# Sixty-four experts on one core: router, slots and first gathers moved under the shared expert, and the residual rows loaded first at the end

## The chip, the core and the metric

The kernel runs on one core of one Trainium2 chip. The metric is the device time of one execution in microseconds, the median of the runs. TensorE (PE) multiplies, VectorE (DVE) and ScalarE (ACT) work elementwise, GpSimd (POOL) and SyncE (SP) issue DMAs, each from a queue of its own, and all transfers run on the core's 16 DMA engines. Each engine runs its own instruction stream in order, and streams meet at semaphores.

## The reference

Two blocks follow each other on 512 tokens of width 1024, in fp32. The first has a state-space mixer, a convolution mixer and two dense feed-forwards, the second a hybrid mixer, cross attention to 256 memory rows, and a mixture of experts. The change touches only the second block from its cross attention on:

```python
x = layer_norm_2(DEEPNORM_ALPHA * x + xa, ln2_g[l], ln2_b[l])
ff = moe_ffn(x, w_router, router_bias, w_exp_gu, w_exp_down, w_sh_gu, w_sh_down)
x = layer_norm_2(DEEPNORM_ALPHA * x + ff, ln3_g[l], ln3_b[l])

def moe_ffn(x2d, ...):
    scores = sigmoid(x2d @ w_router)                     # 512 x 64
    sel = scores + router_bias                           # the best 4 of 8 groups, then the best 8 experts
    w = scores[top_idx] / sum(...) * 2.5
    # every expert: swiglu(rows of its tokens, w_exp_gu[e], w_exp_down[e]) * w, added to its tokens
    return routed + swiglu(x2d, w_sh_gu, w_sh_down)      # one shared expert for all tokens
```

An expert's gate/up weights are 1024 x 512 (2048 KB), its down weights 256 x 1024 (1024 KB).

## The kernel before, in words

Everything is written by hand, engine by engine; the order of the code is the order of each engine's stream. `phase_end` is a barrier: every engine signals that it is drained and waits for the others. SP's loads of weights go through two ring buffers (`wring0`, `wring1`), a load being issued when PE has finished the tiles that used the buffer (`tile_done`). PE's results of a tile go to one of four PSUM banks, which ACT evacuates (`take`, `take_raw`, with `tile_evac`).

The mixture begins behind barrier 16, with the normalised state transposed (features on partitions) in `hT`. PE multiplies it with the router weights (line 1472), turns `hT` back to token rows (`turn`, 8 tiles), then does the shared expert's gate/up (`proj_pairs`, 4 tiles), its down product (`proj`, 8 tiles) and turns the residual `ALPHA*hT + shared` from `sq` to rows (8 tiles). ACT computes the sigmoid (2107), waits for DVE's choice of experts and weights, writes the weights' high part (2109), and then copies the row tiles into two buffers `tokb`, which POOL writes to DRAM tables one by one, each write waiting for the one before: first `xtab` (the rows that experts gather), later `rest` (the residual rows). A barrier (17) follows. Then PE multiplies the 0/1 choice mask with a triangle and with ones, to get each token's position in its expert's list (lines 1489 to 1494), then another barrier (18), then for experts 0 to 2 the slots: DVE makes a one-hot matrix (`m_onehot`), PE multiplies it with the table `rinfo` of token numbers, ranks and weights (`m_idx`), DVE converts the result to indices (`m_conv`), and POOL gathers the expert's rows, at most 112 (`m_gather`).

The expert loop has one step per expert (`m_step`). Every fp32 operand is split into a high and a low fp32r part, and a product is three products of parts. PE turns the gathered rows (`m_turn`), ACT and DVE split them (`m_xhi`, `m_xlo`) and the gate/up weights (`m_ghi`, `m_glo`, four slices each), PE multiplies (`m_gu`, 24 matmuls), ACT and DVE apply silu and the token's weight (`m_silu`, `m_act`), and so on to the down product (`m_down`) and POOL's scatter of the result (`m_scatter`) to row rank x 512 + token of `ytab`: an expert that is a token's r-th writes to rank r's 512 rows. Weight buffers are four deep: `wgu` (here `wring0`, `wring1`, `uT`, `sq`) and `wdn` (in the arena). SP loads expert e + 4 as soon as expert e's product is done (`expert_gu`, `expert_down`). The high part of even experts' gate/up weights is held in `hT`.

At the end eight ranks and the residual rows are read back (2048 KB each) and added per token. SP issues them in the order 0, 1, 2, 3, 4, rest, 5, 6, 7, each when its buffer is free and all experts that can write to it have scattered (`all_added`). DVE adds ranks 1, 2, 3 and rest onto rank 0; PE adds ranks 4, 5, 6, that sum and rank 7 in PSUM, by products with the identity (`add_rank`, line 1600). The last layer norm and the output follow, 128 rows at a time.

Of the kernel before, what the change touches and what calls it, by code (L numbers as in the profile page):

```python
# [28 lines left out]
ALU = mybir.AluOpType  # L29
# [3 lines left out]
P = 128  # L33
# [107 lines left out]
def build(nc, A, out):  # L141

    ctx = ExitStack()
    with ctx:
# [79 lines left out]
        def pc(name, i=0):  # L224
# [190 lines left out]
        NE, CAP, NTOK, RING, TOPK = 64, 112, T, 8, 8  # L415
        MORE = -(-(NTOK - CAP) // CAP)
# [9 lines left out]
        wgu = (wring[0], wring[1], flat(uT), flat(sq))  # L426
        wgu_lo = (wlo[0], wlo[1], flat(uT_r), flat(sq_r))
# [39 lines left out]
        ranks = carve(TC * NE)  # L467

        rows4 = lambda a: a.rearrange("p (c d) -> p c d", d=D)
        start_of = lambda a, n: arena[:, a:a + n]  # L470
        rank_rows = [rows4(r) for r in (
            wring[0][:, :], wring[1][:, :], flat(uT), flat(hT), flat(sq),
            start_of(moe_top, 4 * D), start_of(10 * D, 4 * D), start_of(moe_top + SLOT, 4 * D))]
        rest_rows = rows4(start_of(2 * D, 4 * D))
        g3, b3 = [[raw[2 * k + half][:, 0:512] for half in range(2)] for k in range(2)]
        fin = [rank_rows[0][:, c, :] for c in range(TC)]
# [25 lines left out]
        iot_and_rot = sem("iot_and_rot")  # L502
# [26 lines left out]
        first_ranks, second_ranks = sem("first_ranks"), sem("second_ranks")  # L529
# [25 lines left out]
        gw_in = [sem(f"group_weights_in{q}") for q in range(4)]  # L555
# [20 lines left out]
        def _(sp):  # L576
# [179 lines left out]
            sp.dma_start(memk, A["mem_2"][0].rearrange("(c p) d -> p c d", p=P)).then_inc(in3, 16)  # L756
            tiles.inc(NK)
# [4 lines left out]

            slot(4, two_cols(A["w_sh_gu_2"][0], 0, 256, 256))
# [3 lines left out]
            sp.dma_start(wrt, A["w_router_2"][0].rearrange("(k p) n -> p k n", p=P)).then_inc(in3, 16)  # L767
            sp.dma_start(rbias, A["router_bias_2"][0].partition_broadcast(P)).then_inc(in3, 16)
            sp.dma_start(sc_c2, A["shape_constants"]).then_inc(in3, 16)
# [45 lines left out]
            def load_rest():  # L815
                sp.dma_start(rest_rows, rest.rearrange("(c p) d -> p c d", p=P)).then_inc(second_ranks, 16)
# [11 lines left out]
            with sp.If(crowded > CAP):  # L828
                for e in done:
                    sp.wait_ge(done[e], 19)  # L830
# [2327 lines left out]
```

## Time and profile before

| | us |
|---|---|
| median of 3 runs | 3196.72 |
| lowest, highest | 3195.97, 3205.72 |
| the profiled execution | 3201.49 |
| its span, first to last instruction | 3199.8 |
| PE, DVE, ACT busy | 2880.4, 2120.2, 1456.7 |

The profile is one execution. Engine rows give the start, the duration, the line, the operation with output<-inputs, and in brackets the engine's idle time before it and what ended that. An x behind a row is a count of merged instructions; an fp32 matmul makes two records. PEclk is the granted share of TensorE's full clock (1.00 is 2.4 GHz, 0.50 is 1.2). DMA share is the mean busy share of the 16 DMA engines.

### The profile page before, as it was taken

To read this page: it belongs to the slowest core of one execution; us is meant where nothing else is said; L and a number is where in the kernel's file an instruction comes from. 1 tells how busy PE (TensorE), PEld (TensorE's weight loads), DVE (VectorE), ACT (ScalarE), POOL (GpSimd) and SP (SyncE) were. 2 spreads that over 40 slices of the span, in tenths; PEclk is the share of its full clock that TensorE was granted. 3 is DMA by queue.
4 is the path that set the end of the run, shared out by engine and by line. 5 is a ranking of instruction groups with operands and counts; after the bars stand their busy time and mean duration, and the time that the engine had idled before them with its cause. 6 is when DMAs were issued, how large, how long until landed. Compare 5 with 4: busy or idle time off the path is not lost.

```text
span 3199.8 us, 36554 instructions
## 1 busy us (share of the span) xinstructions
PE 2880.4 (90%) x12311; PEld 2100.3 (66%) x12311; DVE 2120.2 (66%) x3288; ACT 1456.7 (46%) x2217; POOL 168.6 (5%) x165
## 2 busy tenths in 40 slices
PE   8999899999989899999888998888865999999996
PEld 6777777887868578878664333554444777777773
DVE  4778546776279667762554997431424999999985
ACT  5665432223245532232233554331323887777771
POOL 0000000000000000000000000000000322222220
PEclk9999999999999999999898998989976999999998
DMA  3222222322321022323221000203006999999996
GB/s 106 61 56 68 87 79 79 105 79 81 90 79 53 27 92 92 105 65 107 64 79 50 1 1 24 72 24 118 27 31 240 348 337 342 350 344 340 336 341 263
DMA packets 294316, 419.34 MB, mean 131 GB/s; under 512 B 33643, under 2 KB 178467, under 8 KB 294211
## 3 DMA queue, kind: packets, MB, share of 16 engines
q1 hardware_dynamic: 276675, 380.20, 35.9%
q0 software_dynamic: 17536, 37.78, 3.4%
q8 instruction: 61, 1.00, 0.1%
q14 instruction: 44, 0.36, 0.0%
HBM read 407.42 MB, written 35.65 MB: 138 GB/s over the span
## 4 chain that ended last, share of the span: by engine, by line
PE 61%; SPq 17%; DVE 11%; ACT 4%; DMA 4%; issue 3%; DVEq 0%; ACTq 0%; POOLq 0%
PE tp L1045 37%; SPq L779 12%; PE tp L1004 5%; SPq L786 4%; PE tp L1098 2%; PE tp L1099 1%; PE tp L1100 1%; PE tp L1358 1%; PE mp L1078 1%; PE mp L1064 1%; DVE wring_r L2235 1%; DMA arena<-ytab 1%; PE mp L1273 1%; PE mp L1272 1%; PE mp L1274 1%
## 5 line engine op out<-in xcount | busy, mean ns | idle before, releaser
L1045 PE MATMUL tp<-sq_r,arena_r 128*128 128x512 f32 x1152 | 461.2, 400 | 43.4 <-DVE uT_r L2248 25.7
L1045 PE MATMUL tp<-uT_r,arena_r 128*128 128x512 f32 x1152 | 459.2, 399 | 0.0
L1045 PE MATMUL tp<-sq_r,wring_r 128*128 128x512 f32 x1152 | 459.1, 399 | 0.0
L1045 PEld LDWEIGHTS tp<-sq_r,arena_r 128*128 128x128 f32 x1152 | 218.9, 190 | 104.6 <-issue 48.6
L1045 PEld LDWEIGHTS tp<-uT_r,arena_r 128*128 128x128 f32 x1152 | 219.4, 190 | 54.0 <-issue 1.9
L1045 PEld LDWEIGHTS tp<-sq_r,wring_r 128*128 128x128 f32 x1152 | 219.0, 190 | 49.1
L1045 PE MATMUL tp<-arena_r,wring_r 128*128 128x512 f32 x608 | 243.0, 400 | 0.0
L2235 DVE TENSOR_TENSOR wring_r<-wring,arena_r 128x2048 fp32r<-128x2048 f32 x80 | 179.6, 2286 | 79.5 <-ACT arena_r L1652 79.4
L1652 ACT ACTIVATE arena_r<-wring 128x2048 fp32r<-128x2048 f32 x80 | 148.5, 1904 | 56.2 <-DMA wring<-in_w_in 21.7
L1045 PE MATMUL tp<-arena_r,sq_r 128*128 128x512 f32 x480 | 154.8, 404 | 19.6 <-DVE arena_r L2248 19.6
L1871 ACT ACTIVATE arena<-arena 128x512 f32<-128x512 f32 x44 | 27.8, 632 | 291.1 <-DVE arena L2316 291.0
L1045 PE MATMUL tp<-arena_r,uT_r 128*128 128x512 f32 x480 | 151.9, 398 | 7.7 <-DVE arena_r L2248 7.7
L1639 ACT ACTIVATE raw<-tp 128x512 f32<-128x512 f32 x74 | 43.9, 598 | 251.1 <-PE tp L1045 182.6
L3038 DVE TENSOR_TENSOR arena_r<-arena,arena_r 128x1024 fp32r<-128x1024 f32 x128 | 150.4, 1216 | 0.9 <-ACT arena_r L2154 0.9
L2316 DVE SCALAR_TENSOR_TENSOR arena<-raw,pcol,arena 128x512 f32<-128x512 f32 x176 | 132.3, 752 | 24.3 <-DVE arena L2316 6.1
L1098 PE MATMUL tp<-sq_r,wring_r 128*128 128x512 f32 x320 | 133.7, 418 | 8.7 <-issue 8.7
L1045 PEld LDWEIGHTS tp<-arena_r,wring_r 128*128 128x128 f32 x608 | 116.1, 191 | 27.7
L1100 PE MATMUL tp<-sq_r,wring_r 128*128 128x512 f32 x320 | 129.6, 405 | 0.0
L1099 PE MATMUL tp<-uT_r,wring_r 128*128 128x512 f32 x320 | 129.4, 404 | 0.0
L2154 ACT ACTIVATE arena_r<-arena 128x1024 fp32r<-128x1024 f32 x128 | 127.9, 1051 | 0.0
L1045 PEld LDWEIGHTS tp<-arena_r,sq_r 128*128 128x128 f32 x480 | 93.0, 195 | 43.1 <-issue 12.5
L941 POOL DMA_INDIRECT ytab<-arena x64 | 94.8, 1480 | 461.6 <-ACT arena L2171 454.7
(464 smaller groups left out, 6253.3 us busy)
## 6 DMA issues: line engine op xcount, KB each, us to landing
arena<-in_w_exp_down SPq DMA_DIRECT2D x64, 1024.0 KB
wring<-in_w_exp_gu SPq DMA_DIRECT2D x64, 768.0 KB
uT<-in_w_exp_gu SPq DMA_DIRECT2D x32, 768.0 KB
sq<-in_w_exp_gu SPq DMA_DIRECT2D x32, 768.0 KB
wring<-in_f_up_w SPq DMA_DIRECT2D x22, 1024.0 KB, 5.2
wring<-in_f_up_w SPq DMA_DIRECT2D x44, 512.0 KB, 6.7
wring<-in_w_exp_gu SPq DMA_DIRECT2D x32, 512.0 KB
wring<-in_f_down_w SPq DMA_DIRECT2D x32, 448.0 KB, 5.6
```

The source lines that it names most:

```text
L779: sp.dma_start(dst[:, a:z, :], gu[:, a:z, :]).then_inc(wg_ready[b], 16)
L786: sp.dma_start(wdn[b].rearrange("p (k n) -> p k n", n=D), dn).then_inc(wd_ready[b], 16)
L1004: ins = nc.tensor.matmul(b[lo:hi, 0:n], w, x, start=k == 0, stop=k == len(mms) - 1)
L1045: ins = nc.tensor.matmul(b[:], parts[wp][:, kk, m * P:(m + 1) * P], xparts[xp][:, kk, :], start=n_k == 0 and q == 0, stop=n_k == k - 1 and ...
L1098: nc.tensor.matmul(bank[:], w_hi[:, kk, cs], u_hi[1][:, kk, :], start=kk == 0, stop=False)
L1099: nc.tensor.matmul(bank[:], w_hi[:, kk, cs], u_lo[1][:, kk, :], start=False, stop=False)
L1100: ins = nc.tensor.matmul(bank[:], w_lo[:, kk, cs], u_hi[1][:, kk, :], start=False, stop=kk == NK - 1)
L1652: nc.scalar.activation(hi[r][1][:, a:b], wring[r][:, a:b], ACT.Copy).then_inc(whi_ready, 1)
L2154: nc.scalar.activation(wdn_hi[b][:, s], wdn[q][:, s], ACT.Copy).then_inc(moe["dhi"], 1)
L2235: V.tensor_tensor(wlo[r][:, a:b], wring[r][:, a:b], hi[r][1][:, a:b].bitcast(F32), ALU.subtract).then_inc(wlo_ready, 1)
L2316: ins = V.scalar_tensor_tensor(dst, r[:, PAD - t:PAD - t + T], w(taps - 1 - t), dst, ALU.mult, ALU.add)
L3038: V.tensor_tensor(wdn_lo[q][:, s], wdn[q][:, s], wdn_hi[b][:, s].bitcast(F32), ALU.subtract).then_inc(moe["dlo"], 1)
```

## The change

Five edits.

1. The router's weights, bias and constants are loaded with the memory rows, far ahead, and PE's wait for them moves there.
2. ACT copies the token rows before it waits for the routing weights. The rows have four buffers for `xtab` and four for `rest`, so that the writes don't wait for each other. All `rest` rows must have landed (`tok_out`) before SP loads the down weights of experts 2 and 3 into the same memory.
3. Barriers 17 and 18 are gone. PE's position products stand between the shared gate/up and the shared down, `m_idx` of experts 0 to 2 between tiles of the shared down, DVE's and POOL's parts accordingly. POOL issues the first two gathers before the `rest` writes, the third behind them.
4. `wgu` is rotated to `uT`, `wring1`, `wring0`, `sq`. Expert 0's gate/up and the down weights of 0 and 1 are loaded at barrier 16, expert 1's gate/up after the shared gate/up, expert 2's after the shared down, expert 3's after the residual rows are turned. In the first step ACT and DVE split the gathered rows before the weights.
5. At the end the residual rows are loaded first, into `uT`, as the base of DVE's sum, then ranks 0 to 7. DVE adds 0, 1, 2, 3; PE still adds 4, 5, 6, the sum, 7.

```diff
@@ buffers
-        wgu = (wring[0], wring[1], flat(uT), flat(sq))
+        wgu = (flat(uT), wring[SH_GU_SLOT], wring[1 - SH_GU_SLOT], flat(sq))
+        row_tok = [arena[:, (14 + c) * D:(15 + c) * D] for c in range(2)] + tokb
+        row_rest = [arena[:, (4 + c) * D:(5 + c) * D] for c in range(TC)]
@@ SP
             sp.dma_start(memk, A["mem_2"][0].rearrange("(c p) d -> p c d", p=P)).then_inc(in3, 16)
+            sp.dma_start(wrt, A["w_router_2"][0].rearrange("(k p) n -> p k n", p=P)).then_inc(in3, 16)
+            sp.dma_start(rbias, A["router_bias_2"][0].partition_broadcast(P)).then_inc(in3, 16)
+            sp.dma_start(sc_c2, A["shape_constants"]).then_inc(in3, 16)
...
-            sp.wait_ge(tile_done, tiles.v)
-            for e in range(2):
-                expert_gu(e, e)
-                expert_down(e, e)
-            for e in done:
-                sp.wait_ge(done[e], 17)
+            assert tiles.v == RES_TILES
+            expert_gu(0, 0)
+            expert_down(0, 0)
+            expert_down(1, 1)
+            sp.wait_ge(tile_done, RES_TILES - 8)
+            expert_gu(1, 1)
+            sp.wait_ge(tile_done, RES_TILES)
+            expert_gu(2, 2)
+            sp.wait_ge(tile_done, RES_TILES + 8)
+            expert_gu(3, 3)
+            sp.wait_ge(tok_out, 16 * 2 * TC)
             for e in range(2, 4):
-                expert_gu(e, e)
                 expert_down(e, e)
@@ POOL
+            for c in range(TC):
+                pool.wait_ge(tile_evac, TOK_TILES + 2 * c + 2)
+                G.dma_start(xtab[c * P:(c + 1) * P, :], row_tok[c]).then_inc(tok_out, 16)
+            pool.wait_ge(tok_out, 16 * TC)
...
-            for e in range(3):
-                m_gather(e, e % 2, e)
+            for e in range(2):
+                m_gather(e, e, e)
+            for c in range(TC):
+                pool.wait_ge(tile_evac, RES_TILES + 2 * c + 2)
+                G.dma_start(rest[c * P:(c + 1) * P, :], row_rest[c]).then_inc(tok_out, 16)
+            m_gather(2, 0, 2)
@@ PE
-            pe.wait_ge(in3, 16 * 12)
...
-            for e in range(3):
-                m_idx(e, e, e % 2)
+            pe.wait_ge(glu_ready, 2 + 2 * FFN_TILES + 8 + 8 + 2)
+            w = slot_wait()[:, 0:2 * D].rearrange("p (k n) -> p k n", n=D)
+            for m in range(NK):
+                tile([(w[:, k, m * P:(m + 1) * P], sact[:, k, :]) for k in range(2)])
+                if m in (1, 3, 5):
+                    m_idx(m // 2, m // 2, m // 2 % 2)
...
+            pe.wait_ge(tile_evac, RES_TILES + 8)
             m_turn(0, 0, 16)
@@ ACT
             nc.scalar.activation(scr, mp[0][:, 0:TC * NE], ACT.Sigmoid).then_inc(rt["scores"], 1)
+            take_rows(row_tok)
             act.wait_ge(rt["weights"], 1)
             nc.scalar.activation(rinfo[:, :, 2:3], rtmp.unsqueeze(2), ACT.Copy).then_inc(rt["weights_hi"], 1)
-            take_rows(range(TC))
@@ DVE, the sums at the end
-            dve.wait_ge(first_ranks, 16 * (4 + 2))
-            for c in range(TC):
-                add_rows(c, rank_rows[1])
-            dve.wait_ge(second_ranks, 16 * 3)
-            for c in range(TC):
-                for rows in (rank_rows[2], rank_rows[3]):
-                    add_rows(c, rows)
-                add_rows(c, rest_rows, last=True)
+            dve.wait_ge(first_ranks, 16 * (4 + 1))
+            for r in range(4):
+                dve.wait_ge(early_ranks[r], 48 * 10 + 16)
+                for c in range(TC):
+                    add_rows(c, rank_rows[r], last=r == 3)
```

PE between the shared down product (`proj`, L1004) and the first expert's rows, before: `mp1` and `mp2` hold the positions, `ident,sq` is the turn of the residual.

```order
L1016 MATMUL tp2<-ident,sq 128x128 [waits tile_evac]
L1016 MATMUL tp2<-ident,sq 128x128 x3
L1491 MATMUL mp1<-arena,stri 128x64 [waits pool_done,dve_done,act_done]
L1490 MATMUL mp1<-arena,ones 128x64
L1491 MATMUL mp1<-arena,stri 128x64
L1490 MATMUL mp1<-arena,ones 128x64 x2
L1491 MATMUL mp1<-arena,stri 128x64
L1490 MATMUL mp1<-arena,ones 128x64 x3
L1491 MATMUL mp1<-arena,stri 128x64
L1493 MATMUL mp2<-arena,ones 128x64 x4
L1509 MATMUL mp1<-arena_r 128x6 [waits pool_done,moe_onehot,dve_done,act_done]
L1509 MATMUL mp1<-arena_r 128x6 x3
```

And now, from the last position product on (L1505 is `m_idx`, L1010 the shared down):

```order
L1490 MATMUL mp2<-arena,ones 128x64 x4
L1010 MATMUL tp3<-arena,wring0 128x512 [waits tile_evac,w_ready0,glu_ready]
L1010 MATMUL tp3<-arena,wring0 128x512
L1010 MATMUL tp0<-arena,wring0 128x512 [waits tile_evac]
L1010 MATMUL tp0<-arena,wring0 128x512
L1505 MATMUL mp1<-arena_r 128x6 [waits moe_onehot]
L1505 MATMUL mp1<-arena_r 128x6 x3
L1010 MATMUL tp1<-arena,wring0 128x512 [waits tile_evac]
L1010 MATMUL tp1<-arena,wring0 128x512
```

The positions stood behind the turned residual and a barrier, the first slots behind a second one; both stand ahead of or inside the shared down now, and no wait names another engine's barrier.

SP's queue from barrier 16 on, before (`uT`, `sq`, `wring` take gate/up weights, `arena` the down weights):

```order
L767 DMA arena<-in_w_router_2 128x8x64 [waits dve_done,pool_done,act_done,pe_done]
L768 DMA arena<-in_router_bias_2 128x64
L769 DMA arena<-in_shape_constants 128x68
L779 DMA wring0<-in_w_exp_gu_2 128x3x512 [waits tile_done]
L779 DMA wring0<-in_w_exp_gu_2 128x3x512
L779 DMA wring0<-in_w_exp_gu_2 128x2x512
L786 DMA arena<-in_w_exp_down_2 128x2x1024
L779 DMA wring1<-in_w_exp_gu_2 128x3x512 x2
L779 DMA wring1<-in_w_exp_gu_2 128x2x512
L786 DMA arena<-in_w_exp_down_2 128x2x1024
L779 DMA uT<-in_w_exp_gu_2 128x3x512 [waits dve_done,pool_done,act_done,pe_done]
```

And now:

```order
L784 DMA uT<-in_w_exp_gu_2 128x3x512 [waits dve_done,pool_done,act_done,pe_done]
L784 DMA uT<-in_w_exp_gu_2 128x3x512
L784 DMA uT<-in_w_exp_gu_2 128x2x512
L791 DMA arena<-in_w_exp_down_2 128x2x1024 x2
L784 DMA wring1<-in_w_exp_gu_2 128x3x512 [waits tile_done]
L784 DMA wring1<-in_w_exp_gu_2 128x3x512
L784 DMA wring1<-in_w_exp_gu_2 128x2x512
L784 DMA wring0<-in_w_exp_gu_2 128x3x512 [waits tile_done]
```

Three loads come directly behind the barrier, where the router's constants were, and the others one by one as buffers come free.

SP's queue at the end, before:

```order
L813 DMA wring0<-ytab 128x4x1024 [waits scattered1,scattered0,moe_gu]
L813 DMA wring1<-ytab 128x4x1024 [waits scattered1,scattered0,moe_gu]
L813 DMA uT<-ytab 128x4x1024 [waits scattered1,scattered0,moe_gu]
L813 DMA hT<-ytab 128x4x1024 [waits scattered1,scattered0]
L813 DMA sq<-ytab 128x4x1024 [waits scattered1,scattered0,moe_gu]
L816 DMA arena<-rest 128x4x1024 [waits moe_down]
L813 DMA arena<-ytab 128x4x1024 [waits scattered1,scattered0] x2
L821 DMA arena<-ytab 128x1024 [waits scattered1,scattered0,moe_down]
```

And now:

```order
L825 DMA uT<-rest 128x4x1024 [waits moe_gu]
L822 DMA wring1<-ytab 128x4x1024 [waits scattered1,scattered0,moe_gu]
L822 DMA wring0<-ytab 128x4x1024 [waits scattered1,scattered0,moe_gu]
L822 DMA hT<-ytab 128x4x1024 [waits scattered1,scattered0]
L822 DMA sq<-ytab 128x4x1024 [waits scattered1,scattered0,moe_gu]
L822 DMA arena<-ytab 128x4x1024 [waits scattered1,scattered0] x2
L822 DMA arena<-ytab 128x4x1024 [waits scattered1,scattered0,moe_down]
L830 DMA arena<-ytab 128x1024 [waits scattered1,scattered0,moe_down]
```

The residual rows moved from the sixth place to the first, and ranks 0 to 4 each went one place back.

## Rows read from the trace of the kernel before

**Rows 1.** The page, the chain that ended last: shares by engine.

```profile
PE 61%; SPq 17%; DVE 11%; ACT 4%; DMA 4%; issue 3%; DVEq 0%; ACTq 0%; POOLq 0%
```

**Rows 2.** Windows: stretch, length, busy of each engine, PEclk, DMA share, GB/s.

```profile
2410.40:2471.60 61.20, 25.43 (x119) 22.28 (x120) 20.67 (x45) 14.49 (x22) 6.16 (x8) 0.58 0.77 277
2471.60:2495.00 23.40, 23.05 (x123) 18.15 (x122) 22.40 (x34) 20.63 (x31) 5.76 (x4) 1.00 0.89 298
2495.00:2640.00 145.00, 145.00 (x730) 112.68 (x729) 142.66 (x222) 121.87 (x174) 43.70 (x30) 1.00 1.00 346
2640.00:3100.00 460.00, 427.71 (x2144) 331.96 (x2143) 419.20 (x642) 347.63 (x514) 98.94 (x86) 1.00 0.99 342
3100.00:3164.00 64.00, 42.61 (x169) 28.10 (x168) 36.88 (x41) 29.04 (x43) 5.72 (x5) 0.87 1.00 386
```

**Rows 3.** Timeline of SP's queue: start, us, line, what is loaded.

```profile
2410.39 1.44 SPq L779 DMA_DIRECT2D wring<-in_w_exp_gu  x3
...
2437.68 3.04 SPq L779 DMA_DIRECT2D uT<-in_w_exp_gu  x3
...
2471.58 8.77 SPq L779 DMA_DIRECT2D wring<-in_w_exp_gu  x6
```

**Rows 4.** Timeline from the router to the shared down product, several engines.

```profile
2330.93 0.37 SPq L767 DMA_DIRECT2D arena<-in_w_router  x1
...
2334.81 13.88 PE L1472 MATMUL mp<-arena,hT 128*128 128x64 f32 x64 [14.26 <-DMA arena<-in_shape_constants]
...
2350.09 0.39 ACT L2107 ACTIVATE arena<-mp 128x256 f32<-128x256 f32 x1
...
2361.18 0.65 ACT L2109 ACTIVATE arena_r<-arena 128x256 fp32r<-128x256 f32 x1 [10.71 <-DVE arena L2957]
...
2362.31 3.67 PE L1016 MATMUL tp<-ident,hT 128*128 128x128 f32 x16 [10.21 <-ACT arena L1639]
...
2367.01 27.70 PE L1004 MATMUL tp<-hT,wring 128*128 128x512 f32 x64 [1.02 <-ACT arena L1639]
...
2396.35 14.01 PE L1004 MATMUL tp<-arena,wring 128*128 128x512 f32 x32 [1.63 <-DVEq L2970]
...
2400.78 0.69 DVE L2974 SCALAR_TENSOR_TENSOR sq<-hT,raw 128x512 f32<-128x512 f32 x1 [1.02 <-ACT raw L1639]
```

**Rows 5.** Timeline: residual rows, positions, and one index product in the loop.

```profile
2412.59 2.07 ACT L1639 ACTIVATE arena<-tp 128x512 f32<-128x512 f32 x4 [1.54 <-PE tp L1016]
...
2422.78 0.53 POOL L922 DMA_DIRECT2D rest<-arena  x1 [8.28 <-DMA rest<-arena]
...
2433.93 0.53 POOL L922 DMA_DIRECT2D rest<-arena  x1 [3.06 <-DMA rest<-arena]
...
2437.74 0.66 PE L1491 MATMUL mp<-arena,stri 128*128 128x64 f32 x2 [22.18 <-ACTq L569]
...
2442.03 1.91 PE L1493 MATMUL mp<-arena,ones 128*128 128x64 f32 x8
...
2472.08 0.59 PE L1509 MATMUL mp<-arena_r 128*128 128x6 f32 x4
```

**Rows 6.** Timeline: low parts of expert 1's weights, and its first product.

```profile
2465.56 4.62 DVE L3032 TENSOR_TENSOR wring_r<-wring,arena_r 128x1024 fp32r<-128x1024 f32 x4
...
2472.72 0.47 PE L1528 MATMUL tp<-arena_r 128*112 128x512 f32 x1
```

**Rows 7.** Timeline of PE's sums at the end.

```profile
3153.84 5.95 PE L1600 MATMUL tp<-sq,ident 128*128 128x512 f32 x8 [15.12 <-DMA sq<-ytab]
3159.63 3.60 PE L1600 MATMUL mp<-sq,ident 128*128 128x512 f32 x8
3163.98 3.71 PE L1600 MATMUL tp<-arena,ident 128*128 128x512 f32 x8 [0.75 <-DMA arena<-ytab]
...
3172.68 1.88 PE L1600 MATMUL tp<-wring,ident 128*128 128x512 f32 x4
```

**Rows 8.** Timeline of DVE's sums at the end, the first addition behind the residual rows.

```profile
3158.85 1.23 DVE L3107 TENSOR_TENSOR wring<-wring,uT 128x1024 f32<-128x1024 f32 x1 [17.94 <-DMA arena<-rest]
```

More of the change, by code:

```diff
@@ L554, in build @@
         )}
-        gw_in = [sem(f"group_weights_in{q}") for q in range(4)]
+        gw_in = [sem(f"group_weights_and_ranks_in{q}") for q in range(4)]
+        early_ranks = gw_in
         gw_hi, gw_lo, gw_used = sem("group_weights_hi"), sem("group_weights_lo"), sem("group_weights_used")
@@ L829, in _ @@
                 for e in done:
-                    sp.wait_ge(done[e], 19)
+                    sp.wait_ge(done[e], 17)
                 with sp.Fori(0, MORE) as bb:
@@ L1478, in _ @@
             proj_pairs(hT)
-            pe.wait_ge(glu_ready, 2 + 2 * FFN_TILES + 8 + 8 + 2)
-            proj(2, sact, 8)
-            assert tiles.s == RES_TILES
-            pe.wait_ge(conv_ready, NBANK + CONVS)
-            for c in range(TC):
-                for half in range(2):
-                    turn([sq[:, 4 * half + k, c * P:(c + 1) * P] for k in range(4)])
-            phase_end(pe, "pe", ph)
+            pe.wait_ge(rt["weights"], 1)
             for c in range(TC):
@@ L2107, in _, with take_rows @@
             nc.scalar.activation(scr, mp[0][:, 0:TC * NE], ACT.Sigmoid).then_inc(rt["scores"], 1)
+            def take_rows(rows):
+                for row in rows:
+                    for half in range(2):
+                        take(row[:, 512 * half:512 * half + 512])
+            take_rows(row_tok)
             act.wait_ge(rt["weights"], 1)
             nc.scalar.activation(rinfo[:, :, 2:3], rtmp.unsqueeze(2), ACT.Copy).then_inc(rt["weights_hi"], 1)
-            def take_rows(ns):
-                for n in ns:
-                    for half in range(2):
-                        if n >= 2 and half == 0:
-                            act.wait_ge(tok_out, 16 * (n - 1))
-                        take(tokb[n % 2][:, 512 * half:512 * half + 512])
-            take_rows(range(TC))
             for j in range(2):
@@ L2958, in _ @@
             dve.wait_ge(rt["weights_hi"], 1)
+            dve.wait_ge(pool_tables, 1 + 4 + 1)
             V.tensor_tensor(rinfo[:, :, 3:4], rtmp.unsqueeze(2), rinfo[:, :, 2:3].bitcast(F32), ALU.subtract)
+            V.tensor_copy(rinfo[:, :, 0:1], slotid[:, :, 0:1])
+            V.tensor_copy(rinfo[:, :, 4:6], slotid[:, :, 1:2].broadcast_to([P, TC * NE, 2]))
+            for c in range(TC):
+                one = slice(c * NE, (c + 1) * NE)
+                ins = V.tensor_tensor_scan(ranks[:, one], ones[:, 0:NE], mask[:, one], 0.0, ALU.mult, ALU.add)
+            link(ins)
+            V.tensor_scalar(rinfo[:, :, 1:2], ranks.unsqueeze(2), -1.0, float(NTOK), ALU.add, ALU.mult)
             tiles.inc(8)
```

118 lines of the change are left out of this document (49 added, 69 removed).

## The prediction

> **What bounds the kernel now.** I read the chain that ended last first [rows 1]: PE 61%, but 17% is SPq, the DMA queue's own issuing, and 4% DMA. So there is a stretch in which transfers set the pace. The windows show where [rows 2]: from 2495 on the DMA share is 1.00 or 0.99 to 3164, at 342 to 346 GB/s. PE is full up to 2640 (145.00 of 145.00 us) and then starved (427.71 of 460.00). Up to 2640 PE lives on what was loaded ahead; the transfers fall behind all the same. The expert loop therefore ends when its bytes are through. The DMA engines are a server that never rests from 2495 on, and the loop's end moves by exactly what that server gets done earlier or idles less before. In front of it, 2410.4 to 2471.6 has a share of 0.77: 0.23 x 61.2 = 14.1 us idle, 16.95 MB moved (277 GB/s x 61.2). The next 23.4 us have 0.89: 2.6 us idle. Together 16.7 us. The weights of experts 0 to 3 are asked for at 2410.39 and 2437.68, the fifth at 2471.58 [rows 3].
>
> Why the start is so slow can be read engine by engine [rows 4, 5]. PE begins the router at 2334.81 after a load issued at 2330.93. ACT is free at 2350.5 but queued on the routing weights until 2361.18, and PE stands 10.21 us behind it. PE then does shared gate/up (2367.01, 27.70 us) and shared down (2396.35, 14.01 us). Then come the writes of the residual rows, each waiting for the one before (8.28 us for the first), and PE stands 22.18 us until 2437.74 at a barrier.
>
> **The change, PE's side.** (a) Router constants are loaded at the memory stage, so PE waits for the barrier alone. The barrier had fallen when SP issued at 2330.93; PE starts at 2331.2, 3.6 us earlier. (b) ACT takes the eight row tiles before it waits for the weights. PE's eight tiles take twice the 3.67 us of sixteen transposes [rows 4], 7.3 us after the router's 13.88, so shared gate/up starts at 2331.2 + 13.9 + 7.3 = 2352.4 against 2367.01: 14.6 us with (a). The half clock may now fall on its first microseconds, which in the trace fell on the transposes: 0 to 2 us, I take 1. Left: 13.6. (c) The position products move between the two shared products: 2437.74 to 2443.94 [rows 5] is 6.2 us at half clock, 3.1 at full. They cover the 1.63 us wait for the activation, net +1.5. (d) Three index products in the shared down: 0.59 us for four overlapping matmuls, I count 0.45 each, +1.4. DVE's small operations for them go beside PE's 1.75 us tiles (14.01 / 8); a tile leaves DVE 1.02 us idle beside its 0.69 [rows 4], and three of eight tiles get some 1.5 us more, with four raw buffers between: cost 0. Bounds of (d) are 0 and 3 us, if PE had to wait for each. So shared down ends 13.6 - 1.5 - 1.4 = 10.7 us earlier, at 2399.7. (e) No barriers, no serial writes: after the last eight tiles (ACT 0.52 us each [rows 5]) PE turns expert 0's rows, gathered long before. The first split of weights can't start earlier, since its target is hT, which the residual needs: ACT's first slice is ready some 3 us after the copies, an estimate from the turn, the copies of its result and one slice. DVE then makes the low parts of experts 0 and 1 (4.62 us each [rows 6]) with some 3 us of small work, before PE may do expert 1's product: 2401 + 5 + 3 + 9.2 + 3 = 2421, against 2472.72 [rows 6]. PE's side is 51 us ahead there.
>
> **The change, the transfers' side.** Expert 0's gate/up and the down weights of 0 and 1 are asked for at 2331, expert 1's gate/up at the end of the shared gate/up, near 2381: 2048 KB + 2 x 1024 KB + 2048 KB = 6.3 MB, now under idle DMA. At 344 GB/s that is 18.3 us of service taken out. The rest (16.95 - 6.3 = 10.65 MB) starts with expert 2 at 2399.7, and at the 360 GB/s of that window (277 / 0.77) takes 29.6 us, to about 2429. Expert 4, due once expert 0's product is done (about 2417) and SP is free, comes before that, so the queue does not run dry as it did before 2471.58. Gain: 10.7 (earlier start) + 16.7 (idle) + 18.3 (bytes) = 45.7, less what the new start idles. There is a first-byte delay, and a gap where SP waits for all row writes before the down weights of experts 2 and 3: 0 to 6 us, I take 3. Result **42.7 us**. It is below PE's 51, and since the loop waits for transfers [rows 2], the smaller one counts; the other 8 us are turned into earlier starvation.
>
> The new wait on SP (tok_out) has queued behind it two down loads, four small ones and expert 4; ACT and through it PE wait for these. In the trace the first write took 8.28 us beside 6.3 MB of weights, and all four were through near 2437 [rows 5], which is 23 us for 8.4 MB, so the DMA engines lost nothing, only the order. Now about 5 MB stand against the writes, 15 us from 2403: SP is free by 2418. The Trainium skill ("DMA: Bandwidth & Descriptors", section "Queues, rings and completion order") says that each DMA engine goes round-robin between the queues that have work, packet by packet. By that rule the writes on POOL's queue would have half the rate and be through near 2415, and the gap would be nearer 0 than 3; the 8.28 us row (512 KB, 63 GB/s) shows less than half. The sum is 42.7 by the row and about 45 by the rule.
>
> **The change, the end.** Nine loads of 2 MB are served in a row, and three landings lie 5.1 us apart [rows 7, 8]: rank 4 at 3153.8, the residual rows at 3158.85, rank 5 at 3163.9. The DMA share stays at 1.00, so putting the residual rows first adds no byte and removes none: each of ranks 0 to 4 lands one place later, rank 5 and what follows where they did. DVE gets its sums ready sooner (it waited to 3158.85 [rows 8], first sum three additions of 1.23 later), but PE asks for the first only at 3172.68 [rows 7]: no gain. PE's first additions are rank 4's: 5.95 us for the first eight at a mostly halved clock, then 3.60, start to start 9.2 us before it can take rank 5. Before, 3153.84 + 9.2 = 3163.0 lay within the wait for rank 5. Now it is 3158.9 + 9.2 = 3168.1, against 3163.98, and from there PE works without a gap to the end. Price **+4.1 us**. Bounds: 0, if rank 4 lands no later, and +5.1, one whole load.
>
> **Sum.** -42.7 + 4.1 = -38.6 us. Against the profile's own time, 3201.5 (span 3199.8 and 1.7 around it), that is 3162.9. That execution lies 4.8 us above the median of 3196.7, so the median should be **3158.1**.
>
> **Rivals.**
> - PE's pace decides: all 51 us arrive, less 4.1: 3196.7 - 46.9 = 3150. For it: PE full to 2640. Against it: 32 us of starving after that. Chance 0.10.
> - The end costs nothing (rank 4 not late, or the clock up in time): 3154. Chance 0.15.
> - SP stands at tok_out. If the four writes keep the 63 GB/s of the 8.28 us row, 2.1 MB take 33 us, to 2436; the down weights and expert 4 wait, and DMA idles from about 2418, 18 us: 3176. For it: that row. Against it: the writes sped up as soon as the weights were through. Partial forms cost less. Chance 0.12.
> - The change doesn't do what it says: a barrier's work is only moved, DVE's position chain holds PE in the shared down, and the first gather is late again. Then only the earlier bytes (18.3 us) remain, less 4.1: 3182. Chance 0.04.
> - Slower: gathers and scatters share the DMA engines with a queue that is now full from the first expert. If each of the 60 experts lost 0.9 us to a late gather, 54 us would outweigh the 38.6 and give 3212. It decides from 38.6 / 60 = 0.65 us per expert on. Against it: the queue has been just as full from 2495 on with PE at 145.00 of 145.00. Chance 0.03.
> - The forecast, 3154.5 to 3163: chance 0.56.
>
> **How the numbers follow.** The likeliest case gives 3158.1. The range reaches from the PE-paced case (3149) to a partly stalled SP (3170) and leaves out the deep stall, the undone change and the slowdown, with a little on the other side. A measurement of this kernel can tell about 0.3%, 9.6 us, from no change. Faster by more: 0.96; within: 0.01; slower by more: 0.03.
>
> **What would show it.** Shared gate/up should start near 2352 and shared down end near 2400 (a to d); expert 1's product near 2421 (e). The DMA share from 2400 to 2440 should be above 0.9, and expert 4's load issued by 2424. If the loop's windows show PE starved soon after 2500 rather than 2640, the transfers decide, as I hold; if they show PE full for as long as before, the first rival does. At the end PE should first wait for rank 4 and then run without a gap, some 4 us later against the last expert's end. Wrong would be: DMA idle behind tok_out, a PE gap inside the shared down over 1 us, or an expert period above 10.7 us.

## The result, and the profile after

Beside each other on one chip, the changed kernel took 3152.64 us (median of four, 3148.13 to 3155.74) and the kernel before 3196.62. The ratio is 0.9847, with a 95% interval from 0.9833 to 0.9861: 48.9 us less, between 44.4 and 53.4. From the 3196.7 us that the prediction started from this gives 3147.8 (3143.3 to 3152.3), against a forecast of 3158.1: 10.3 us lower, and 1.2 below the low end of the range (3149). How far below the forecast it lies is not known that well. The two medians by themselves are 44.0 us apart, and the traces below give 46.4, which would be 3150.3. By every one of these figures the gain is larger than the 38.6 us forecast. The direction and both mechanisms came as forecast. The gain at the start was some 8 us larger.

The profiled execution after took 3154.16 us, with a span of 3152.4. What lies ahead of the last barrier varies from run to run: in the 14 traces of this document the barrier falls between 2321.90 and 2333.77 us, and not by kernel. So I measure from that barrier. POOL's first IOTA (the instruction that writes a row of counting numbers) behind it marks when it fell. Timelines of POOL, SP and PE in the changed kernel (start, us, engine, line, operation, tiles; in brackets the wait before it and who ended it):

```profile
2329.48 0.24 POOL L918 IOTA arena<- 128x128 f32 x1 [603.98 <-ACTq L573]
...
2343.13 5.86 PE L1022 MATMUL tp<-ident,hT 128*128 128x128 f32 x32
...
2348.82 27.63 PE L1010 MATMUL tp<-hT,wring 128*128 128x512 f32 x64
...
2394.70 1.43 SPq L784 DMA_DIRECT2D wring<-in_w_exp_gu  x3
...
2396.15 3.71 PE L1022 MATMUL tp<-ident,sq 128*128 128x128 f32 x32 [1.48 <-DVE sq L3063]
...
2399.89 2.99 SPq L784 DMA_DIRECT2D sq<-in_w_exp_gu  x3
...
2405.27 0.45 PE L1524 MATMUL tp<-hT_r,arena_r 128*112 128x512 f32 x1
...
2411.45 0.88 SPq L791 DMA_DIRECT2D arena<-in_w_exp_down  x2
...
2414.31 6.43 SPq L784 DMA_DIRECT2D uT<-in_w_exp_gu  x3
...
2416.12 0.75 PE L1524 MATMUL tp<-arena_r 128*112 128x512 f32 x1
```

In these rows the router's tiles are turned in one go. There is no gap between them and the shared gate/up product (2348.82, before 2367.01 in [rows 4]). The whole block of weights before expert 4 has been asked for by 2412.3, and expert 4 follows at 2414.31 (before 2471.58, [rows 3]). Expert 0's product starts at 2405.27 and expert 1's at 2416.12 (before 2472.72, [rows 6]). The index products of three experts lie inside the shared down product, and the gathers of experts 0 and 1 beside it:

```profile
2382.46 0.90 PE L1505 MATMUL mp<-arena_r 128*128 128x6 f32 x4
...
2384.96 1.32 POOL L937 DMA_INDIRECT arena<-xtab,arena  x1 [34.40 <-DVE arena L3010]
...
2388.76 1.34 POOL L937 DMA_INDIRECT arena<-xtab,arena  x1 [2.49 <-DVE arena L3010]
```

Windows of the changed kernel (stretch, length, busy time of PE, weight loads, DVE, ACT and POOL, PEclk, DMA share, GB/s), which answer to [rows 2]:

```profile
2330.00:2360.00 30.00, 30.00 (x122) 23.78 (x122) 12.22 (x69) 8.36 (x13) 3.16 (x7) 0.71 0.54 211
2360.00:2400.00 40.00, 38.38 (x143) 21.02 (x141) 12.19 (x30) 9.73 (x18) 3.81 (x4) 1.00 0.29 99
2395.00:2400.00 5.00, 3.71 (x32) 3.48 (x32) 0.69 (x1) 3.52 (x8) 1.15 (x2) 1.00 0.76 263
2400.00:2495.00 95.00, 89.99 (x447) 69.92 (x448) 91.24 (x139) 78.53 (x111) 17.89 (x19) 0.96 1.02 359
2495.00:2640.00 145.00, 138.46 (x693) 107.53 (x691) 133.16 (x206) 110.88 (x163) 31.64 (x28) 0.99 0.99 339
2640.00:3048.00 408.00, 379.40 (x1900) 294.32 (x1899) 372.70 (x570) 309.44 (x457) 87.64 (x76) 1.00 0.99 343
```

The DMA engines hardly rest from 2400 on (a share of 0.99 or more), where before they idled 16.7 us after 2410. PE is starved in 2495 to 2640 (138.46 of 145.00), where before it was full (145.00). That is the sign that the prediction named for "the transfers decide". By 2495 the DMA engines had been busy 0.54 x 30 + 0.29 x 40 + 95 = 122.8 us since the barrier. In the kernel before it was 75.1 us. One new row of the kernel before and two of [rows 2] give that: 0.09 x 79.4 + 0.77 x 61.2 + 0.89 x 23.4.

```profile
2331.00:2410.40 79.40, 62.69 (x192) 38.25 (x192) 16.68 (x71) 14.23 (x23) 3.56 (x9) 0.78 0.09 31
```

The difference is 47.7 us, 49.6 if the share of 1.02 is taken as it stands. Of that 1.5 us are the earlier barrier. The bytes say it more plainly. These are the first 165.5 us behind the barrier in the kernel before, in the changed one, and in late_loads, a kernel that comes below (the last figure of each row is GB/s):

```profile
2330.98:2496.48 165.50, 112.65 (x437) 79.75 (x438) 61.17 (x156) 50.83 (x77) 16.28 (x21) 0.74 0.46 163
2329.48:2494.98 165.50, 158.88 (x711) 115.22 (x712) 115.63 (x238) 96.63 (x141) 25.28 (x32) 0.92 0.75 268
2333.77:2499.27 165.50, 148.43 (x654) 107.15 (x655) 103.35 (x220) 85.45 (x126) 26.43 (x30) 0.89 0.66 236
```

268 against 163 GB/s over 165.5 us is 17.4 MB more. At the 341 GB/s at which the rest of the loop runs that is 51 us. Behind 2495 the two kernels run at nearly the same rate: 346 and 339 GB/s up to 2640, then 342 and 343.

At the end, PE's sums and DVE's, timeline of the changed kernel:

```profile
3054.04 4.94 SPq L791 DMA_DIRECT2D arena<-in_w_exp_down  x2
...
3101.28 4.63 DVE L3108 TENSOR_TENSOR uT<-uT,sq 128x1024 f32<-128x1024 f32 x4 [0.45 <-DMA sq<-ytab]
...
3107.45 6.04 PE L1606 MATMUL tp<-arena,ident 128*128 128x512 f32 x8 [21.00 <-DMA arena<-ytab]
3113.32 3.60 PE L1606 MATMUL mp<-arena,ident 128*128 128x512 f32 x8
3116.76 3.60 PE L1606 MATMUL tp<-arena,ident 128*128 128x512 f32 x8
...
3128.98 1.30 DVE L3124 BATCH_NORM_STATS2 arena<-tp 128x6 f32<-128x512 f32 x2 [23.07 <-PE tp L1606]
```

PE first waits for rank 4 and then runs through to its last product at 3142.52: rank 5's additions no longer have a wait of their own, as in [rows 7], but follow rank 4's at 3116.76. DVE's sums are through by 3105.9 and then DVE stands idle for 23.07 us. The last down weights are asked for at 3054.04, and at 3105.69 in the kernel before:

```profile
3105.69 5.25 SPq L786 DMA_DIRECT2D arena<-in_w_exp_down  x2
```

That request divides every kernel below into two parts: **loop** (from the barrier to it) and **end** (from it to the end of the span). Both are read in each kernel's own trace, in us. The first product is expert 0's. The median is that of all runs of the kernel:

```
kernel        barrier to       loop    end    both    median   ratio to the kernel before,
              first product                                     with 95% interval
before           132.1         774.7   94.1   868.8   3196.6
tail_new         132.2         779.7   98.2   877.9   3207.0   1.0011 (0.9997 to 1.0024)
after             75.8         724.6   98.4   822.9   3152.6   0.9847 (0.9833 to 0.9861)
after_again       75.7         729.0   97.8   826.8   3153.8   0.9852 (0.9836 to 0.9869)
pe_up             75.9         725.2   98.2   823.4   3148.8   0.9844 (0.9828 to 0.9861)
tail_old          75.7         725.1   93.3   818.4   3148.9   0.9835 (0.9818 to 0.9852)
dve_six           75.7         727.9   94.9   822.8   3150.8   0.9838 (0.9821 to 0.9856)
dve_seven         75.8         725.3   93.2   818.5   3150.9   0.9843 (0.9824 to 0.9862)
rt_late           79.7         730.4   99.0   829.4   3156.1   0.9862 (0.9837 to 0.9886)
rest_serial       75.9         731.4   98.6   830.0   3159.4   0.9883 (0.9862 to 0.9904)
gather_late       90.0         737.9   98.5   836.5   3160.7   0.9869 (0.9851 to 0.9886)
act_late          88.6         739.7   97.9   837.6   3165.7   0.9895 (0.9875 to 0.9914)
late_loads        78.3         741.6   98.4   840.0   3167.7   0.9891 (0.9874 to 0.9908)
bytes_up          75.9         745.4   98.4   843.8   3177.8   0.9932 (0.9915 to 0.9949)
```

The kernel before had medians of 3199.4 to 3203.3 beside the other groups, so the ratios are what can be compared. Below, "timed" is a ratio's distance from 0.985, the changed kernel's in two groups, times 3197 us. An interval of 0.0017 on either side is 5 us, so the traces are the sharper measure, and the timed figure is there to bear them out.

Six kernels share the start and the loop traffic of the changed one. Their loops lie between 724.6 and 729.0, mean 726.2. The two with the old start have 774.7 and 779.7, mean 777.2. So a loop is known to some 2.5 us, the two traces of the changed kernel itself lie 4.4 apart, and the change moved the loop by **51.0 us**. The ends with the old order take 93.3 and 94.1, and those with the new order and PE's old work 97.8 to 99.0, mean 98.3: **+4.6 us**. Together that is 46.4, within the interval of the timed ratio.

### The profile page after: what moved, and what is told of

Read it like the earlier page. It is cut to its first block, busy times and chain, and to the rows that moved or that the text cites. A ratio compares the mean times of both kernels' runs of the same rounds, so it can differ in the third digit from the quotient of the medians.

```text
span 3152.4 us, 36525 instructions
## 1 busy us (share of the span) xinstructions
PE 2867.7 (91%) x12311; PEld 2089.4 (66%) x12311; DVE 2120.3 (67%) x3288; ACT 1455.4 (46%) x2217; POOL 154.8 (5%) x165
## 4 chain that ended last, share of the span: by engine, by line
PE 61%; SPq 18%; DVE 11%; ACT 4%; DMA 3%; issue 3%; DVEq 0%; ACTq 0%; POOLq 0%
PE tp L1051 37%; SPq L784 12%; PE tp L1010 5%; SPq L791 4%; PE tp L1104 1%; PE tp L1364 1%; PE tp L1105 1%; PE tp L1106 1%; PE mp L1084 1%; PE mp L1070 1%; DMA arena<-ytab 1%; DVE wring_r L2237 1%; PE mp L1279 1%; PE mp L1278 1%; PE mp L1280 1%
## 5 line engine op out<-in xcount | busy, mean ns | idle before, releaser
L2314 DVE TENSOR_TENSOR raw<-tp,rinv 128x512 f32<-128x512 f32 x88 | 60.6, 688 | 83.5 <-PE tp L1051 83.2
```

## The experiments

### Who sets the loop's pace

The theory is that the loop is a row of transfers, so that bytes cost time and PE work does not. The rival is that PE, busy 93% of the time, sets the pace. One kernel adds only bytes, one adds only PE work, and one moves bytes back.

**More bytes** (bytes_up). Edit, once with expert 4's load and once with each gate/up load in the hardware loop:

```diff
+                sp.dma_start(pick(spare.rearrange("e p k n -> p e k n"), e), gu[:, 0:1, 0:256]).then_inc(spare_in, 16)
```

> The changed kernel with 57 more transfers in the expert loop, one of 128 KB with each load of gate/up weights (DRAM to DRAM, read by no one), 7.47 MB in all, and no more work for any engine. Transfers set the loop's end: 7.47 MB at 344 GB/s = 21.7 us later than the changed kernel, 3174 (some more, to 28 us, if a copy costs the DMA engines more than a load). PE sets it: PE idles 6 to 7 us of 100 in the loop, 0 to 5 us later.

Measured: loop 745.4, which is 19.2 us above 726.2; timed +26 us. 21.7 had been forecast, and it lies between the two. Windows of bytes_up:

```profile
2495.00:2640.00 145.00, 133.61 (x676) 103.92 (x675) 130.55 (x200) 108.62 (x161) 30.23 (x27) 1.00 0.98 342
2640.00:3000.00 360.00, 329.36 (x1614) 254.88 (x1613) 316.82 (x486) 262.55 (x385) 72.98 (x66) 0.98 0.99 342
```

The DMA share and the rate stay as they were, and PE simply waits more (329.36 of 360.00).

**More PE work** (pe_up). Edit, in each half of every down product:

```diff
                         a_hi, a_lo = act_hi[:, k, 0:CAP], act_lo[:, k, 0:CAP]
+                        if k == 0:
+                            nc.tensor.matmul(mp[2 + half][0:CAP, :], a_hi, hi[:, k, s], start=True, stop=True)
```

> The changed kernel with two matmuls more in every expert's down product (one of 512 columns for each half, its result overwritten by the next), 2 x 0.235 us x 64 = 30 us of PE work and no byte more. Transfers set the loop's end: PE idles 0.7 us per expert, which takes it in: 0 to 3 us later than the changed kernel, 3153 to 3156. PE sets it: 25 to 30 us later, 3178 to 3183.

Measured: loop 725.2, not above the mean of the others; timed -2 us. Windows of pe_up:

```profile
2495.00:2640.00 145.00, 145.00 (x734) 112.87 (x733) 138.03 (x214) 117.78 (x169) 28.46 (x29) 1.00 0.97 337
2640.00:3000.00 360.00, 349.55 (x1739) 270.93 (x1738) 327.71 (x502) 271.72 (x399) 77.45 (x68) 1.00 0.99 341
```

30 us of PE work went into PE's gaps and the loop did not notice. The first rival of the prediction, PE's pace, falls. The gaps are nearly full with it, though: PE is busy for 349.55 of 360.00 us. What more work than that would cost was not tried.

**The early loads undone** (late_loads). Edit:

```diff
+            sp.wait_ge(tile_done, RES_TILES)
             expert_gu(0, 0)
             expert_down(0, 0)
+            expert_gu(1, 1)
             expert_down(1, 1)
-            sp.wait_ge(tile_done, RES_TILES - 8)
-            expert_gu(1, 1)
-            sp.wait_ge(tile_done, RES_TILES)
             expert_gu(2, 2)
```

> Only one part undone: the weights of experts 0 and 1 are asked for when the shared down product is done (as before the change) and not at the barrier and after the shared gate/up. 6.3 MB go from idle DMA time back into the busy stretch. Transfers set the loop's end (my theory): 6.3 MB at 344 GB/s = 18.3 us later than the changed kernel, 3171. PE sets it (rival): PE only waits for expert 0's 3 MB at the start, 3 MB / 344 GB/s = 9 us from 2396 against a first product at 2405, so 0 to 3 us later, 3153 to 3156.

Measured: loop +15.4 us, timed +13. The first product comes only 2.5 us later, so PE's side can't explain it. The transfers can. By its row above, 236 GB/s instead of 268, this kernel has moved 5.3 MB less by 165.5 us behind the barrier, which is 15.5 us at 341 GB/s. It is less than the 6.3 MB, 18.3 us, that I counted, since this kernel then moves a little more per us (365 GB/s in the 95 us from 2400 on, and the changed one 359); why it does is not shown.

### The steps of the start, one undone in each kernel

**Router constants** (rt_late). Edit:

```diff
                 sp.wait_ge(done[e], 16)
+            sp.dma_start(wrt, A["w_router_2"][0].rearrange("(k p) n -> p k n", p=P)).then_inc(in3, 16)
+            sp.dma_start(rbias, A["router_bias_2"][0].partition_broadcast(P)).then_inc(in3, 16)
+            sp.dma_start(sc_c2, A["shape_constants"]).then_inc(in3, 16)
```

(and taken away at the memory stage; PE waits for them before the router).

> The changed kernel with the router's three loads asked for after the barrier again. Term (a) of the prediction: PE starts the router 3.6 us later, all that follows it up to the loop starts later too, with the transfers: 3.6 us later than the changed kernel (0 to 4.5). If the start doesn't matter: 0.

Measured: first product 3.9 us later, as forecast. The loop is +4.2 and timed +4, which fits; but 730.4 is only 1.4 us above the second trace of the changed kernel, so the loop alone would not show it.

**ScalarE's row tiles before the routing weights** (act_late). Edit:

```diff
-            take_rows(row_tok)
             act.wait_ge(rt["weights"], 1)
             nc.scalar.activation(rinfo[:, :, 2:3], rtmp.unsqueeze(2), ACT.Copy).then_inc(rt["weights_hi"], 1)
+            take_rows(row_tok)
```

> The changed kernel with ScalarE's eight row tiles again behind its wait for the routing weights. PE's turn of the rows waits for the banks until about 2356 to 2362: shared gate/up starts 8 to 11 us later than at 2348.82, after a longer rest at half clock, and DVE's chain stays as it is. Transfers set the end and start with the shared down product: 8 to 11 us later than the changed kernel, 3161 to 3164. If the loads of experts 0 and 1 that are already in were enough to cover it: 0 to 3 us.

Measured: loop +13.5, timed +14, where 8 to 11 were expected. The wait of [rows 4], 10.21 us, is back to the hundredth. Timeline of act_late, the second half of the turned rows:

```profile
2353.71 3.28 ACT L1645 ACTIVATE arena<-tp 128x512 f32<-128x512 f32 x6
...
2354.38 3.67 PE L1022 MATMUL tp<-ident,hT 128*128 128x128 f32 x16 [10.21 <-ACT arena L1645]
```

From barrier to shared gate/up it is 30.9 us here and 19.3 in the changed kernel, so this one reordering is worth 11.6 us on PE, and the shared down product then starts 12.1 us later. I had booked 11.0 for it, less 1 for the clock.

**The first gathers before the residual rows** (gather_late). Edit:

```diff
-            for e in range(2):
-                m_gather(e, e, e)
             for c in range(TC):
                 pool.wait_ge(tile_evac, RES_TILES + 2 * c + 2)
                 G.dma_start(rest[c * P:(c + 1) * P, :], row_rest[c]).then_inc(tok_out, 16)
+            for e in range(2):
+                m_gather(e, e, e)
```

> The changed kernel with the gathers of experts 0 and 1 behind the writes of the residual rows (as before the change) and not under the shared down product. 0.92 MB go back into the busy stretch, and PE's first expert waits: the last write is issued at 2401.7, a gather takes some 8 us to land, so PE's first turn comes near 2410 instead of 2400.9. Transfers set the loop's end: 0.92 MB / 344 GB/s = 2.7 us later, 3155. PE sets it: 8 to 9 us later, 3161.

Measured: loop +11.7, timed +6. By the trace this is above what either theory had said (2.7, and 8 to 9), by the timed ratio between them, and it corrects the way I had put them against each other. PE's first product comes 14.2 us later: the first gather is issued at 2402.88, behind the four writes and not at 2384.96, and PE's turn follows 11.5 us after it, with the DMA engines full (a share of 1.03 from 2400 to 2420). Timelines of PE and SP in gather_late, and one of its windows:

```profile
2414.41 1.73 PE L1513 MATMUL tp<-ident,arena 112*128 112x112 f32 x8 [13.74 <-DMA arena<-xtab,arena]
...
2427.59 1.45 SPq L784 DMA_DIRECT2D uT<-in_w_exp_gu  x3
```

```profile
2420.00:2440.00 20.00, 18.63 (x90) 14.48 (x90) 19.86 (x31) 16.19 (x22) 1.96 (x2) 0.91 0.75 265
```

Expert 4's load is asked for at 2427.59 instead of 2414.31, because it waits for the buffer that expert 0's product frees. By then the queue has run dry: 0.25 x 20 = 5.0 us idle. With 2.7 us for 0.92 MB served later this makes 7.7 us, and the bytes moved by 165.5 us behind the barrier (254 against 268 GB/s, 2.3 MB) make 6.8. The other 4 to 5 us of the trace lie in a slower stretch behind, 338 GB/s against 339 to 341 in the equal kernels. What slows it is not shown, and the timed figure does without it. PE's work costs nothing in this loop, but **the moment of PE's first product** does, as it is what releases the next load.

**The residual rows written one after the other** (rest_serial). Edit:

```diff
                 pool.wait_ge(tile_evac, RES_TILES + 2 * c + 2)
+                if c:
+                    pool.wait_ge(tok_out, 16 * (TC + c))
```

> The changed kernel with the four writes of the residual rows one after the other, each waiting for the one before (as before the change). It is the deep stall at the new wait of SP made real: down weights 2 and 3 and expert 4 are asked for only when the fourth write has landed. By the 8.28 us of a first write and 3.06 us of a later one in the kernel before, SP passes between 2415 and 2431 instead of 2411.45. The queue holds about 6 MB at 2400, so it runs dry near 2418. Transfers set the end: 0 us if SP passes by 2418, and one us for every us after it, up to 13 us; I expect SP at 2423 and 3 to 6 us later than the changed kernel. If neither the writes nor that wait matter: 0.

Measured: loop +5.2, timed +11 (within 7 or so either way); 3 to 6 had been expected. POOL's and SP's timelines in rest_serial, whose barrier fell at 2321.90, and its windows behind them:

```profile
2390.75 0.61 POOL L959 DMA_DIRECT2D rest<-arena  x1 [8.12 <-ACT arena L1647]
2398.47 0.55 POOL L959 DMA_DIRECT2D rest<-arena  x1 [7.11 <-DMA rest<-arena]
2404.73 0.53 POOL L959 DMA_DIRECT2D rest<-arena  x1 [5.72 <-DMA rest<-arena]
2408.18 0.53 POOL L959 DMA_DIRECT2D rest<-arena  x1 [2.91 <-DMA rest<-arena]
...
2411.12 0.90 SPq L791 DMA_DIRECT2D arena<-in_w_exp_down  x2
```

```profile
2400.00:2405.00 5.00, 5.00 (x19) 3.48 (x17) 4.93 (x10) 3.89 (x5) 0.27 (x1) 0.83 0.65 251
2405.00:2410.00 5.00, 0.14 (x1) 0.00 (x0) 5.00 (x6) 2.28 (x3) 1.76 (x3) 0.85 0.40 165
2410.00:2415.00 5.00, 0.00 (x0) 0.00 (x0) 0.57 (x1) 0.00 (x0) 2.49 (x2) 0.50 0.65 211
```

SP passes its new wait 89.2 us behind the barrier and not 82.0, and the DMA engines idle 1.75 + 3.0 + 1.75 = 6.5 us. So the rival "SP stands at tok_out" is a real mechanism at 5 to 6 us, and what avoids it in the changed kernel is that the four writes go out together. There they are issued from 2398.22 on and are through at 2411.45: 2.1 MB in 13.2 us, 159 GB/s, beside loads in a queue that moves about 360 in all. The prediction had taken 23 us for the old serial writes and 15 for these.

### The end

**The new end on the kernel before** (tail_new), and **the old end on the changed kernel** (tail_old). The edit is the part of the change that concerns the last loads and sums, applied or undone; its core in tail_old:

```diff
-                load_rest()
...
                 load_rank(4, late_ranks[0])
+                sp.wait_ge(moe["down"], NE - 1)
+                load_rest()
```

> The kernel before with the changed end alone (residual rows first, ranks 0 to 5 one place later, DVE's and PE's sums in the new order). My theory: rank 4 lands one load (5.1 us) later, PE's first additions go with it, 4 us later than the kernel before: 3200.7 (bounds 0 and +5.1). Rival: the order of equal loads costs nothing, 3196.6.

> The changed kernel with the old end (residual rows after rank 4). My theory: the start keeps its 50 us and the end gives 4.1 to 4.6 us back: 3148 against 3152.6. Rival (the end is free): 3152.6.

Measured: the end takes 98.2 us in tail_new against 94.1, and 93.3 in tail_old against 98.3. Timed, tail_new is 3.5 us above the kernel before (between -1 and +8) and tail_old 5 below the changed kernel, neither clear of zero by itself. The traces decide it, since ends of one order repeat closely (93.3 and 94.1, and 97.8 to 99.0): residual rows first cost 4 to 5 us. Timeline of PE in tail_old:

```profile
3101.93 5.28 PE L1605 MATMUL tp<-sq,ident 128*128 128x512 f32 x8 [14.99 <-DMA sq<-ytab]
...
3112.01 3.71 PE L1605 MATMUL tp<-arena,ident 128*128 128x512 f32 x8 [1.37 <-DMA arena<-ytab]
```

Rank 4 is there 47.4 us behind the last down-weight request (3101.93 - 3054.50), and in the changed kernel 53.4 us (3107.45 - 3054.04).

**DVE takes more of the sums.** DVE stood idle 23 us in the new end, so it can take work from PE. In dve_six it adds ranks 4 and 5, and in dve_seven also rank 6 for three of the four row blocks. Core of the edits:

```diff
-            for r in range(4):
-                dve.wait_ge(early_ranks[r], 48 * 10 + 16)
-                for c in range(TC):
-                    add_rows(c, rank_rows[r], last=r == 3)
+            for r in range(7):
...
+                for c in range(1 if r == 6 else 0, TC):
+                    add_rows(c, rank_rows[r], last=r == (6 if c else 5))
```

> The changed kernel, but DVE also adds ranks 4 and 5, and PE adds only rank 6, DVE's sums and rank 7. DVE stood 23 us at the end after its sums; four additions of 1.2 us for rank 4 and four for rank 5 end about 5 us after rank 5 lands, some 4 us before rank 6. My theory: PE's 9.2 us of half-clock additions leave the chain, which then goes by rank 6's and 7's landing: 3 to 5 us earlier than the changed kernel, 3148 to 3150. Rival: PE's clock is low for rank 6 and 7 because it had nothing to do before them, and the additions of rank 6 to 7 take twice as long: 0 to 4 us later, 3153 to 3157.

> The changed kernel, with DVE adding ranks 4 and 5 and three of the four row blocks of rank 6 as well; PE adds rank 6 of one block, DVE's sums and rank 7. In the kernel in which DVE took ranks 4 and 5, the end from the last down-weight request became 94.9 instead of 98.3 us. PE's work after rank 6 has landed is 24 groups of 0.43 x 2 us (20.6 us for four blocks); three blocks less rank 6 take 3 x 1.72 = 5.2 us off that, and DVE's three additions (3.7 us) end before PE wants them, if DVE's norms then follow PE no worse. My theory: 89.8 us for the end, 8.5 us less than the changed kernel: 3144. Rival: the norms and output copies on DVE set the pace after rank 7, then 3 to 4 us less only: 3149.

Measured: the end is 94.9 in dve_six (3.4 less, as forecast) and 93.2 in dve_seven (5.1 less and not 8.5). In dve_six PE's half clock does not go away, it moves to rank 6: its first four products, behind 30 us of rest, take 3.75 us at a granted clock of 0.50, and 1.88 later on.

```profile
3122.90 3.75 PE L1606 MATMUL tp<-arena,ident 128*128 128x512 f32 x4 [29.95 <-DMA arena<-ytab]
```

In dve_seven the mechanism of its rival shows, though it gave 3 to 4 us: with PE relieved, DVE's norms follow one another without a wait for PE. Timeline of DVE in dve_seven:

```profile
3126.31 1.30 DVE L3122 BATCH_NORM_STATS2 arena<-tp 128x6 f32<-128x512 f32 x2 [4.60 <-PE tp L1606]
...
3131.19 1.29 DVE L3122 BATCH_NORM_STATS2 arena<-tp 128x6 f32<-128x512 f32 x2
...
3136.06 1.29 DVE L3122 BATCH_NORM_STATS2 arena<-mp 128x6 f32<-128x512 f32 x2
...
3140.93 1.29 DVE L3122 BATCH_NORM_STATS2 arena<-mp 128x6 f32<-128x512 f32 x2
```

4.88 us lie from block to block, against 5.15 in the changed kernel, where PE set the pace (six groups of 0.86), so three blocks save under a microsecond. dve_seven (818.5 us behind the barrier) and tail_old (818.4) are the shortest by their traces, some 5 us below the changed kernel; their timed ratios, 0.9843 and 0.9835, can't be told from its 0.985.

## Why the prediction was right and where it was not

- **The smaller of two sums counts, and it is the transfers'.** Right. pe_up adds 30 us of PE work for nothing, and bytes_up pays for its bytes. PE's side was ahead by 55.1 us at expert 1's product (2472.72 - 2416.12, less 1.5 for the earlier barrier), against 51 forecast, and the loop took 51.0 of it. The slack between the two is not 8 us but 4, and gather_late shows that the two sums are not independent. That the loop gained just the 51 us that the first rival had for PE's pace is chance: pe_up excludes that rival.
- **The step that failed is the size of the transfers' sum: 42.7 forecast, 51.0 measured** (50.1 in the pair of profiles compared here). Three of its terms were too small, by 3.5, 1.8 and 2.7 us, together 8.0. By its terms:
  - *Earlier start*, 10.7 forecast. Expert 2's load is asked for at 2394.70, where the first load stood at 2410.39 in [rows 3]: 15.7, less 1.5 for the barrier, 14.2. Terms (c) and (d) held: 1.3 and 1.3 us against 1.5 and 1.4. What was mis-sized is (b): I took the 32 transposes at twice the half-clock row of 16, 7.3 us, and 1 us more for a half clock on the gate/up. They took 5.86, as the granted clock was 0.60 there and not 0.50, and the gate/up its full-speed 27.63. With 0.3 in (a) that is about 3 of the 3.5 us.
  - *New idle*, 3 forecast. The rows show 0.24 x 5 = 1.2 us before 2400 and none behind. SP got past the wait at 2411.45 and not at 2418. That is 1.8 us.
  - *Bytes served early*, 18.3 forecast. Two gathers of 112 rows (0.92 MB, 2.7 us) also left the busy stretch. I had moved them in the argument on PE and forgot them in the one on DMA: 18.3 + 2.7 = 21.0.
  - *Idle of the old start*, 16.7: gone entirely, as booked.
  - Together 14.2 + 16.7 + 21.0 - 1.2 = 50.7 us, against 50.1 and 51.0 measured, and 51 by the bytes. The kernels that undo one step each don't test these terms singly: gather_late costs 11.7 us where its bytes are 2.7, so the steps lean on each other. No run puts the barriers 17 and 18 back alone.
- **The wait for tok_out.** The 3 us were the middle of a guess from 0 to 6. The rival's deep stall took the 8.28 us of the first write for a rate that four writes would keep (63 GB/s), and that was wrong: rest_serial's chained writes take 7.7, 6.3 and 3.5 us from issue to issue, while the same four together make 159 GB/s. The sum had given the four writes 15 us (2403 to 2418). The round robin of the Trainium skill ("DMA: Bandwidth & Descriptors", section "Queues, rings and completion order"), which the prediction weighed, gave them 12 (2403 to 2415) and a gap nearer 0. The trace has 13.2, between the two, and no gap behind 2400 (a share of 1.02). It does not show in which order the engines took the packets. SP is past the wait at 2411.45 mostly because the writes began 5 us earlier than forecast, at 2398.22.
- **The end**, +4.1 forecast: +4.6 measured. Right, by the mechanism given: rank 4 lands one load later, and PE's first additions come behind it, at a granted clock of 0.59 for the first eight (9.3 us start to start, 3107.45 to 3116.76, where the prediction had 9.2).
- **Rivals.** PE's pace: excluded by pe_up. A free end: excluded by tail_new and tail_old. SP at the wait: 5 to 6 us when provoked (rest_serial), but absent in the changed kernel. Change not effective, or slower by late gathers: no sign. Behind 2495 PE is starved sooner, and the rates are nearly those of before.
- What stays open: the loops of equal kernels spread over 4.4 us, at 336 to 339 GB/s from 2495 to 2640 (the kernel before has 346 there). The 2.5 us by which the trace of bytes_up fell short of its bytes are not told apart from that, nor are the 4 to 5 us of gather_late. Each edit has one profiled execution, so a loop difference of 5 us or less is weak by itself.

## What to carry to other kernels

Where a loop waits for transfers, count for each edit ahead of it what the DMA engines serve earlier and what they idle less, gathers and scatters included, and treat PE's work as free as far as it fits PE's gaps (here 0.47 us per expert did). But look up which PE instruction releases the next load: its start time is part of the transfers' chain. Where loads land in a row at a full DMA share, put first only what an engine on the chain to the end is waiting for; a tensor that is only needed last costs those behind it up to one landing (here 4 to 5 us of 5.1).

## What the runs showed of the chip that I had not expected

- TensorE's clock rose inside an uninterrupted run of small transposes: 32 of them took 5.86 us where 16 at half clock took 3.67 [rows 4]. The granted clock of the stretch is 0.50 up to 2345 and then 0.74. It was at half speed again during expert 0's first product, after 5 us in which PE was busy only 2.17:

```profile
2345.00:2350.00 5.00, 5.00 (x28) 4.40 (x27) 4.49 (x38) 4.27 (x9) 1.90 (x3) 0.74 0.44 172
...
2400.00:2405.00 5.00, 2.17 (x20) 1.99 (x20) 2.26 (x3) 3.92 (x7) 2.09 (x3) 1.00 1.00 361
2405.00:2410.00 5.00, 4.87 (x16) 3.54 (x16) 4.93 (x10) 5.00 (x7) 0.05 (x1) 0.66 1.03 413
```

- A copy from DRAM to DRAM, in pieces of 1 KB, cost the full DMA engines about what a load of the same bytes costs: 7.47 MB in 19.2 us by the loop, 26 by the timed ratio (389 and 284 GB/s, on either side of the loop's own 343).
- Four writes of 512 KB issued together beside a full load queue had 159 GB/s between them, while four in a chain had 68 for the first (512 KB in 7.7 us).
